# The unrounded copies of h at the norms: VectorE and ScalarE four chunks each, GpSimd none

## What is computed

```python
def layer_norm(x, g, b):
    mu = jnp.mean(xf, axis=-1, keepdims=True)
    var = jnp.mean(jnp.square(xf - mu), axis=-1, keepdims=True)
    return ((xf - mu) * lax.rsqrt(var + LN_EPS) * g + b).astype(x.dtype)
...
for l in range(DEPTH):                                  # first block, DEPTH = 2
    h = modulate(x, mod[:, 0, 0], mod[:, 0, 1])         # x * (1 + scale) + shift
    y = swiglu_ffn(h, ffn1_w_in[l], ffn1_w_out[l])
    x = layer_norm(ALPHA * x + 0.5 * mod[:, 0, 2] * y, ln_g[l, 0], ln_b[l, 0])
    ...                                                 # the mixer and a second ffn, each with such a norm
for i in range(DEPTH):                                  # second block: GQA, then MLA attention
    h_lat = x * (1.0 + sc_a) + sh_a
    h_ctx = xc * (1.0 + csc_a) + csh_a
    ...
    x = layer_norm_2(alpha * x + g_a * y_lat, ln_g[i, 0], ln_b[i, 0])
    x = layer_norm_2(alpha * x + g_m * sq_relu_mlp(x * (1.0 + sc_m) + sh_m, mlp_w1[i], mlp_w2[i]), ln_g[i, 1], ln_b[i, 1])
    if need_ctx:
        xc = ...                                        # the same two norms for the context
```

## Time and profile before

| | |
|---|---|
| median of 3 runs | 3721.72 us |
| the profiled execution | 3719.87 us, its span 3718.1 us |
| TensorE matmul busy | 3643.9 us (98%) |
| VectorE busy | 2263.1 us (61%) |
| ScalarE busy | 1711.7 us (46%) |
| GpSimd busy | 727.0 us (20%) |
| granted TensorE clock, mean | 0.994 |

### The profile page before, as it was taken

How to read it: one execution, slowest core, us unless ns; L and a number is a source line. 1 busy time by engine, 2 the same in 40 slices (tenths; PEclk the granted TensorE clock), 3 DMA queues, 4 the chain that set the end, 5 groups by cost and what they waited for, 6 DMA issues and landing times.

```text
span 3718.1 us, 48896 instructions
## 1 busy us (share of the span) xinstructions
PE 3643.9 (98%) x19410; PEld 3076.8 (83%) x19410; DVE 2263.1 (61%) x2742; ACT 1711.7 (46%) x2648; POOL 727.0 (20%) x750
## 2 busy tenths in 40 slices
PE   8999999999999999999999999999999999999998
PEld 6888877888888888788888689888888888988886
DVE  5555766744574567777545488685655467875345
ACT  4444434543454454446433269454544244853223
POOL 2000302300120012032003437550000143642001
PEclk9999999999999999999999999999999999999999
DMA  6454212344344432124332111223332112322221
GB/s 255 183 227 155 84 68 80 148 150 167 136 170 161 167 136 92 46 102 170 147 109 84 42 38 35 77 80 127 123 131 108 51 52 74 78 85 91 102 92 68
DMA packets 71650, 417.37 MB, mean 112 GB/s; under 512 B 8976, under 2 KB 12176, under 8 KB 30480
## 3 DMA queue, kind: packets, MB, share of 16 engines
q1 hardware_dynamic: 70176, 408.19, 30.7%
q10 hardware_dynamic: 1264, 6.29, 0.4%
HBM read 393.48 MB, written 2.10 MB: 106 GB/s over the span
## 4 chain that ended last, share of the span: by engine, by line
PE 88%; DVE 7%; ACT 2%; issue 2%; POOL 1%; DMA 0%; DVEq 0%; SPq 0%; ACTq 0%; POOLq 0%
PE ps L2195 26%; PE ps L2196 25%; PE ps L2197 25%; PE ps L2933 2%; PE ps L2976 2%; DVE x_lat L3403 1%; DVE x_lat L3414 1%; DVE rstd_lat L3391 1%; PE ps L2911 1%; PE ps L2912 1%; DVE w_lo L3072 1%; PE ps L2670 1%; DVE x_lat L3347 0%; DVE h_lo L3424 0%; PE ps L2946 0%
## 5 line engine op out<-in xcount | busy, mean ns | idle before, releaser
L2195 PE MATMUL ps<-h_hi,w_lo 128*128 128x512 f32 (+2 forms) x2872 | 1079.8, 376 | 24.4 <-DVE h_lo L3424 15.3
L2197 PE MATMUL ps<-h_hi,w_hi 128*128 128x512 f32 (+2 forms) x2872 | 1065.0, 371 | 0.0
L2196 PE MATMUL ps<-h_lo,w_hi 128*128 128x512 f32 (+1 forms) x2800 | 1039.3, 371 | 0.0
L3072 DVE TENSOR_TENSOR w_lo<-raw,w_hi 128x2048 fp32r<-128x2048 f32 (+3 forms) x251 | 533.3, 2125 | 654.9 <-ACT w_hi L1423 654.5
L1423 ACT ACTIVATE w_hi<-raw 128x2048 fp32r<-128x2048 f32 (+3 forms) x260 | 454.0, 1746 | 927.2 <-PE ps L2197 908.4
L2195 PEld LDWEIGHTS ps<-h_hi,w_lo 128*128 128x128 f32 (+1 forms) x2872 | 541.4, 188 | 134.3 <-DVE h_lo L3424 24.7
L2197 PEld LDWEIGHTS ps<-h_hi,w_hi 128*128 128x128 f32 (+1 forms) x2872 | 541.4, 189 | 94.3
L2196 PEld LDWEIGHTS ps<-h_lo,w_hi 128*128 128x128 f32 x2800 | 528.2, 189 | 87.8 <-issue 0.5
L2195 PE MATMUL ps<-hid_hi,w_lo 128*128 128x512 f32 (+1 forms) x1272 | 487.7, 383 | 3.9 <-DVE w_lo L3072 2.7
L2196 PE MATMUL ps<-hid_lo,w_hi 128*128 128x512 f32 (+1 forms) x1272 | 483.8, 380 | 0.0
L2197 PE MATMUL ps<-hid_hi,w_hi 128*128 128x512 f32 (+1 forms) x1272 | 483.4, 380 | 0.0
(11 more groups left out here) (523 smaller groups left out, 5799.3 us busy)
## 6 DMA issues: line engine op xcount, KB each, us to landing
raw<-ada SPq DMA_DIRECT2D x113, 1024.0 KB, 4.8
raw<-ffn_in SPq DMA_DIRECT2D x87, 1024.0 KB, 6.7
raw<-mlp_in SPq DMA_DIRECT2D x32, 1024.0 KB, 4.8
raw<-mlp_out SPq DMA_DIRECT2D x32, 1024.0 KB, 4.9
raw<-ffn_out SPq DMA_DIRECT2D x32, 768.0 KB, 4.5
raw<-ffn_out SPq DMA_DIRECT2D x32, 640.0 KB, 3.9
raw<-mix_p SPq DMA_DIRECT2D x14, 1024.0 KB, 4.8
raw<-mix_x SPq DMA_DIRECT2D x8, 1024.0 KB, 4.8
```

The source lines that it names most:

```text
L2195: eng.matmul(out, lo_w, hi_x, start=first, stop=False, skip_group_check=True)
L2196: eng.matmul(out, hi_w, lo_x, start=False, stop=False, skip_group_check=True)
L2197: return eng.matmul(out, hi_w, hi_x, start=False, stop=last, skip_group_check=True)
L3072: eng.tensor_tensor(w_lo[:, slot, 0:ln.width], raw[:, slot, 0:ln.width], w_hi[:, slot, 0:ln.width].bitcast(F32), ALU.subtract).then_inc(s_ ...
```

## The change

GpSimd makes no copy at a norm any more; it still makes those of `context_in`. ScalarE makes chunks 1, 3, 5 and 7. VectorE makes chunks 0, 2, 4 and 6, each directly behind the `scaled` of its group, with a wait for that `scaled` first; the wait is there for group 1 too, which has no chunk for VectorE. GpSimd's `next_x` now follows its sums directly.

```diff
--- before.py
+++ after.py
@@ -22,7 +22,7 @@
 DEPTH = 2
 FF = 2816
 FF_GROUPS = (12, 10)
-ON_ACT = (3, 5, 7)
+ON_ACT = (1, 3, 5, 7)
 BUSY = (1, 2, 8, 0, 0)
 FF2 = 4096
 G2 = 8
@@ -912,7 +912,7 @@
 
             return ps[:, B_SUM[j], 0:HALF]
 
-        def on_pool(norm, k):
+        def off_act(norm, k):
 
             return sum(1 for c in range(k) if not norm.name or c not in ON_ACT)
 
@@ -1153,14 +1153,12 @@
             def modulated(norm):
 
                 eng.wait_ge(s_vec, w.vec + (7 if norm.name else 3) * len(norm.streams))
+                if norm.name:
+                    return
                 for part in norm.parts:
                     x, h32 = X[part.st], sq_h[part.st]
                     g, b, _, _ = affine(norm, part.st)
                     for k in range(DC):
-                        if norm.name:
-                            if k in ON_ACT:
-                                continue
-                            eng.wait_ge(s_v, len(GROUPS) * part.nidx + GROUP_OF[k] + 1)
                         eng.tensor_scalar(h32[:, k, part.cs], x[:, k, part.cs], g[:, k:k + 1], b[:, k:k + 1], ALU.mult,
                                           ALU.add).then_inc(s_n32, 1)
 
@@ -1170,9 +1168,9 @@
                     x = X[part.st]
                     for k in range(DC):
                         eng.wait_ge(s_nhi, DC * part.idx + k + 1)
-                        eng.wait_ge(s_n32, part.n32 + on_pool(norm, k + 1))
-                        if k + 1 > on_pool(norm, k + 1):
-                            eng.wait_ge(s_a32, len(ON_ACT) * part.nidx + k + 1 - on_pool(norm, k + 1))
+                        eng.wait_ge(s_n32, part.n32 + off_act(norm, k + 1))
+                        if k + 1 > off_act(norm, k + 1):
+                            eng.wait_ge(s_a32, len(ON_ACT) * part.nidx + k + 1 - off_act(norm, k + 1))
                         if norm.name:
                             _, _, g, b = affine(norm, part.st)
                             eng.tensor_scalar(x[:, k, part.cs], x[:, k, part.cs], g[:, k:k + 1], b[:, k:k + 1], ALU.mult,
@@ -3413,14 +3411,21 @@
                 eng.wait_ge(s_u, len(GROUPS) * part.nidx + g + 1)
                 eng.tensor_tensor(x, x, rstd[part.st][:, part.cs].unsqueeze(1).broadcast_to([P, n, HALF]), ALU.mult)\
                    .then_inc(s_v, 1)
+                if norm.next:
+                    gain, bias, _, _ = affine(norm, part.st)
+                    eng.wait_ge(s_v, len(GROUPS) * part.nidx + g + 1)
+                    for k in range(k0, k1):
+                        if k not in ON_ACT:
+                            eng.tensor_scalar(sq_h[part.st][:, k, part.cs], X[part.st][:, k, part.cs], gain[:, k:k + 1],
+                                              bias[:, k:k + 1], ALU.mult, ALU.add).then_inc(s_n32, 1)
 
             def split_part(norm, part, g):
 
                 (k0, k1), (hi, lo), h32 = GROUPS[g], H[part.st], sq_h[part.st]
                 eng.wait_ge(s_nhi, DC * part.idx + k1)
-                eng.wait_ge(s_n32, part.n32 + on_pool(norm, k1))
-                if k1 > on_pool(norm, k1):
-                    eng.wait_ge(s_a32, len(ON_ACT) * part.nidx + k1 - on_pool(norm, k1))
+                eng.wait_ge(s_n32, part.n32 + off_act(norm, k1))
+                if k1 > off_act(norm, k1):
+                    eng.wait_ge(s_a32, len(ON_ACT) * part.nidx + k1 - off_act(norm, k1))
                 eng.tensor_tensor(lo[:, k0:k1, part.cs], h32[:, k0:k1, part.cs],
                                   hi[:, k0:k1, part.cs].bitcast(F32), ALU.subtract).then_inc(s_nlo, 1)
 
@@ -3442,6 +3447,8 @@
                 centred(norm, 0, 0)
                 centred(norm, 0, 1)
                 inverse(norm, 0)
+                if norm.next:
+                    eng.wait_ge(s_vec, w.vec + 7 * len(norm.streams))
                 three = len(parts) == 3
                 for j, part in enumerate(parts):
                     scaled(norm, j, 0)
```

## The result

The changed kernel takes 3750.52 us, median of 4 runs (3749.67 to 3755.48), beside 3720.84 us for the kernel before in 4 runs of the same session (3719.10 to 3722.96). The ratio is 1.0082 with a 95% interval of 1.0071 to 1.0094, so the change costs 29.7 us; forecast were 34.4, in a range of 3740 to 3775. The profiled execution has a span of 3747.7 us against 3718.1, 29.6 more, so the traces can be compared term by term.

A forecast was written before the change was run, and what follows sets the result against it. The prediction took VectorE's instruction stream to set each norm's end, in a kernel that is a TensorE matmul stream. Added VectorE work 27.0 plus holds 9.0 less 1.6 made 34.4 us more, 3756 us, range 3740 to 3775.

The forecast's parts named there:

- The price of one copy: On VectorE, a 128x256 tensor_scalar with two per-partition scalars was estimated at 0.41 us, bounds 0.354 and 0.547.
- The insertion: VectorE's new copies and waits add 1.35 us per part before scaled of group 4, 27.0 us over 20 parts.
- The wait: On VectorE, waiting for the scaled just before loses 0.08 us of overlap and adds 0.03: 0.11 us in group 1.
- The holds: GpSimd's x updates, now inside norms, hold VectorE twice per part at 0.25 us: 9.0 us over 18 parts.
- The cover of group 4: Group 4's copy on VectorE, 0.44 us, is hidden by its 1.15 us wait for ScalarE's copy of chunk 7.
- Norm by norm: VectorE's delay: 2.70 us in six common norms and the one before gqa_q, 4.05 in two three-part norms, without holds.
- Updates that hold nobody: GpSimd's x updates find VectorE's gaps in the norms and delay nothing: 3744 to 3747 us; chance 0.22.
- Heavy holding: Each x update holds VectorE 0.56 us: 3767 us, or 3776 if the instruction takes 0.547 too; chance 0.12.
- Its clock part: In the three-part norms, longer TensorE stops may make the granted clock fall in both; within a rival of chance 0.12.
- TensorE's queue as a cover: TensorE's own queue covers the delay of all parts but the last: 12 us, 3734 us; chance 0.04.
- faster: GpSimd's 160 updates leave the units behind the norms, giving back 32 us: 3712 to 3715 us; chance 0.06.
- no difference: Some 110 to 170 holds behind norms vanish against dearer copies, or copies hide behind ScalarE: 3715 to 3729 us; chance 0.06.

The follow-up runs named there:

- copies in halves: The changed kernel with every VectorE copy of 128x256 issued as two of 128x128: 3765.91 us, ratio 1.0126 to the kernel before.
- chunk 6: The kernel before with VectorE copying only chunk 6, behind group 3's split_part; ScalarE copies 1, 3, 5, 7, GpSimd 0, 2, 4: 3718.44 us, ratio 0.9998.
- the updates held: The changed kernel with GpSimd's updates of x held back until the norm's last copy is made: 3745.61 us, ratio 1.0074 to the kernel before.
- such waits alone: The kernel before with only VectorE's wait for its own scaled added behind each scaled of a norm that makes h: 3727.18 us, ratio 1.0018.
- fillers: The changed kernel with 40 matmuls without use in part 1 of each three-part norm, in TensorE's stops: 3753.93 us, ratio 1.0090 to the kernel before.

## Why the prediction was right, step by step

**The bound.** "Inside a norm VectorE's instruction stream sets the end" holds. Additions to it arrive in full (copies in halves), and work in its one slack is free (chunk 6).

**The price of one copy** was worked out as 0.41 from three forms; it is 0.411 at least, and at most 0.416 when no update runs beside it.

**The insertion.** 1.35 us was forecast ahead of `scaled` 4 of each part, so 2.70 at the matmul of rows 3, less the hold of 0.20 on group 2 that goes: 2.50. With the updates held, 2.46 was measured there. The sign named for it, the stretch from the first `scaled` to the end of part 0's last h_lo, grew from 9.19 us to 10.56 (407.41 to 417.97), by 1.37 and not by about 1.9: two holds of 0.13 came, and the old one of 0.20 went, which the 1.9 had left out. My sum ended at this matmul. TensorE then waits for group 3 of the last part too, 0.24 us. The copy of group 4 stands ahead of that h_lo in VectorE's order; I had looked only for what it does to the h_lo of group 4.

**The wait.** Forecast were 0.11 for a wait with nothing behind it and 7.2 us for such waits alone; measured 0.12 and 6.6 (interval 3.3 to 10.0). The Trainium skill ("VectorE: DVE Perf Modes", section "The DRAIN you can't avoid") has a semaphore there for nothing. No run here bears that out. The same section also says that a next instruction which isn't held starts earlier; that is what rows 4 show by 0.08, and what a wait takes away.

**The holds** were mis-sized: 9.0 forecast, 4.9 measured by the medians, 5.9 by the profiled executions and 6.4 by the ledger (6 times 0.73 for the common norms, twice 0.98 for those with three parts). The term took two holds per part at 0.25 each. Part 0 of the first norm has two, on copies, of 0.13 (0.54 against 0.41). Part 1 has more than two, which the prediction had named as a sign that it fails: two copies of 0.54, and ahead of them a `scaled` of 0.68 in place of 0.42 beside an update (VectorE, then GpSimd):

```profile
424.31 0.68 DVE L3412 TENSOR_TENSOR x_lat<-x_lat,rstd_lat 128x256 f32<-128x256 f32 x1
```

```profile
424.16 0.56 POOL L1176 TENSOR_SCALAR x_lat<-x_lat,aff_lat 128x256 f32<-128x256 f32 x1 [5.76 <-ACT h_hi L1654]
```

Together 0.78 in the two parts where 1.0 was taken: more holds than forecast, most of them at half the price. The copies read one tensor, so two reads in SBUF on both engines, of which the prediction speaks, aren't needed for a hold. The whole GpSimd instruction of 0.56, which would be the rule of "SBUF — State Buffer", section "Who interferes with whom", in the Trainium skill, is nowhere added to a row of VectorE in the first norm; beside the copies GpSimd's own instruction grows more, to 0.76 and 0.91. Here the loss is shared.

**The cover of group 4** held in part 0: the wait for ScalarE fell from 1.15 to 0.70. In the last part it held for the last h_lo only, as said.

**Norm by norm**, with the old holds taken off, my sum gives 3.54 for a common norm, 2.5 for the one before gqa_q and 5.3 for each with three parts. The first is right within 0.1 (3.47 on average), from two errors that cancel: 0.2 too little behind group 2, and holds 0.27 too dear (0.73 against 1.0). The norm before gqa_q: the matmul of rows 11 moved by 20.22 us to

```profile
2077.95 0.47 PE L2193 MATMUL ps<-h_hi,w_lo 128*128 128x512 f32 x1 [0.90 <-DVE q_t L3942]
```

while it had been 17.7 late ahead of the norm; so the norm cost 2.5, as forecast, though by another route. On the way TensorE was up to 3.6 late, at a lower clock (0.81 over 2060 to 2078), and 0.63 of it went again at this matmul, whose wait fell from 1.53 to 0.90. What cut the section to 0.54 was the GQA stretch at the better clock, 1.9 us in all. The two others cost 4.7 each at TensorE, and the second had 1.5 given back behind it. So the forecast was over by 4.8 us: about 3.5 by clock that no row of before promised, 2.6 by holds (6 times 0.27, twice 0.52) and 0.3 by the insertion in the three norms that aren't common, less 1.1 that the common norms cost more behind group 2 (6 times 0.2) and 0.43 ahead of the first norm; the rest is rounding. The clock was luck: without it the change would have cost some 33 us.

**The rivals.** Updates that hold nobody (3744 to 3747): refuted by the copies of 0.54, though its time is only 4 us off, and the kernel with the updates held, 3745.6, lands on it. Heavy holding: refuted. Its clock part came true as an event, in both norms with three parts, and cost nothing up to their last h_lo (39.99 and 39.98 with fillers). TensorE's queue as a cover, faster, no difference: refuted by 54 waits of TensorE where there were 25.

## What to carry to other kernels

Find the one engine whose stream sets the end of a stage, and the one wait that it has in it: work moved to that engine costs its full time everywhere but in that wait, however idle the engine is over the span (61% busy here). Price a moved instruction with its lost overlap and its wait, about 0.11 us beside the 0.33 of the copy. Then ask what the engine that was freed does earlier now; its old order was a schedule too.

## What the runs showed of the hardware

- A VectorE instruction behind an independent one starts 0.08 us before that one's end; with a wait for it 0.03 after. A hundred such waits cost 6.6 us.
- A 128x256 tensor_scalar with two per-partition scalars takes 411 ns, 128x128 at least 331, so by an estimate from the two some 250 ns are fixed.
- VectorE and GpSimd, both reading SBUF, slow each other: VectorE by 0.13, 0.20 or 0.26 us per instruction, GpSimd from 0.56 to 0.76 and 0.91. In the changed kernel 5 to 6 of the 29.7 us come from the engine that had been relieved.
- TensorE's stretches at 1.2 GHz wander between kernels whose code there is the same, and were worth 1.5 to 2.9 us each where TensorE sets the time; not all of them have a stop ahead. With matmuls without use in TensorE's waits, one went there and another came 15 us later. Differences of 2 us between such kernels (0.05%) had better be read in the trace norm by norm than in the total.
